# Expert weights of a decoder step loaded as rows of 2048 and 1536 columns, and a visit of two column groups in place of four blocks

## The reference, cut to what matters

```python
def swiglu(x, w_gate, w_up, w_down):
    return (jax.nn.silu(x @ w_gate) * (x @ w_up)) @ w_down

for e in range(N_EXPERTS):                       # 8 experts
    y_e = swiglu(xt, w_gate[e], w_up[e], w_down[e])
    y = y + combine[:, e:e + 1] * y_e
x = layer_norm(ALPHA * x + y, ln2_g, ln2_b)
```

## Time and profile before

| | |
|---|---|
| runs | 1489.25, 1490.39, 1491.16 us |
| profiled execution, span | 1489.3 us |
| what lies around the span | not recorded apart; the span is 1.1 us under the median of the runs |
| TensorE matmul busy | 1403.9 us, 94% |
| VectorE busy | 1323.4 us, 89% |
| ScalarE busy | 1104.7 us, 74% |
| loaded from HBM | 460.79 MB |
| mean granted TensorE clock | 0.986 |

### The profile page before, as it was taken

One profiled execution on the slowest core, in us unless ns is written; L12 is line 12 of the kernel. 1 busy time (PEld: TensorE's weight loads), 2 busy tenths in 40 slices (PEclk: granted clock), 3 DMA queues, 4 the chain that ended last, 5 costly groups with the idle time before them and its releaser, 6 DMA issues.

```text
span 1489.3 us, 39853 instructions
## 1 busy us (share of the span) xinstructions
PE 1403.9 (94%) x17570; PEld 1151.0 (77%) x17570; DVE 1323.4 (89%) x1315; ACT 1104.7 (74%) x1032; POOL 123.7 (8%) x162
## 2 busy tenths in 40 slices
PE   9999999999999999899999999999999898798786
PEld 7788878888788888697777788788877776766563
DVE  3999997555669999899999999999999999999997
ACT  4797755544458766688888878888878988978884
POOL 2411025000143001100000000000000000000001
PEclk9999999999999999999999999999999999999898
DMA  9654558456554637899999999999999999999993
GB/s 315 243 170 157 180 193 269 139 170 239 171 183 141 196 127 266 325 352 386 412 409 395 411 407 395 411 406 402 410 405 412 411 407 411 410 403 410 411 393 133
DMA packets 141347, 464.85 MB, mean 312 GB/s; under 512 B 8234, under 2 KB 10410, under 8 KB 126800
## 3 DMA queue, kind: packets, MB, share of 16 engines
q1 hardware_dynamic: 138960, 457.21, 80.4%
q0 software_dynamic: 1920, 4.55, 1.0%
q10 hardware_dynamic: 288, 0.48, 0.1%
HBM read 460.79 MB, written 2.89 MB: 311 GB/s over the span
## 4 chain that ended last, share of the span: by engine, by line
PE 52%; DVE 34%; DMA 5%; issue 5%; ACT 3%; POOL 1%; DVEq 0%; ACTq 0%
PE ps L869 16%; PE ps L870 16%; PE ps L871 16%; DVE w_lo L2284 14%; DVE w_lo L2287 7%; DMA stage<-in_moe_w_up 2%; PE ps L975 2%; DVE w_lo L1754 2%; ACT w_hi L1663 2%; DMA stage<-in_w_in 1%; DVE arena L1871 1%; DVE arena L1882 1%; POOL x L796 1%; DVE arena L2302 1%; DVE arena L2322 1%
## 5 line engine op out<-in xcount | busy, mean ns | idle before, releaser
L869 PE MATMUL ps<-arena,w_hi 128*128 128x128 f16 (+7 forms) x3952 | 564.5, 214 | 15.0 <-issue 10.1
L870 PE MATMUL ps<-arena,w_hi 128*128 128x128 f16 (+7 forms) x3952 | 564.3, 214 | 7.7 <-issue 7.7
L871 PE MATMUL ps<-arena,w_lo 128*128 128x128 f16 (+7 forms) x3952 | 564.3, 214 | 5.1 <-issue 5.1
L869 PEld LDWEIGHTS ps<-arena,w_hi 128*128 128x128 f16 x3952 | 386.1, 99 | 27.7 <-issue 15.8
L871 PEld LDWEIGHTS ps<-arena,w_lo 128*128 128x128 f16 x3952 | 386.2, 99 | 13.7 <-issue 8.3
L870 PEld LDWEIGHTS ps<-arena,w_hi 128*128 128x128 f16 x3952 | 386.2, 99 | 12.8 <-issue 4.8
L869 PE MATMUL ps<-xhl,w_hi 128*128 128x264 f16 x1088 | 300.4, 276 | 8.9 <-DVE xhl L1812 3.6
L871 PE MATMUL ps<-xhl,w_lo 128*128 128x264 f16 x1088 | 300.3, 276 | 0.0
L870 PE MATMUL ps<-xhl,w_hi 128*128 128x264 f16 x1088 | 300.3, 276 | 0.0
L1754 DVE SCALAR_TENSOR_TENSOR w_lo<-stage,w_hi 128x2048 f16<-128x2048 f32 (+1 forms) x94 | 209.1, 2246 | 80.9 <-ACT w_hi L1359 80.8
L1359 ACT ACTIVATE w_hi<-stage 128x2048 f16<-128x2048 f32 (+1 forms) x94 | 172.2, 1853 | 75.2 <-PE ps L871 62.0
(11 more groups left out here) (339 smaller groups left out, 1973.7 us busy)
## 6 DMA issues: line engine op xcount, KB each, us to landing
stage<-in_moe_w_up SPq DMA_DIRECT2D x64, 1024.0 KB, 14.0
stage<-in_moe_w_down SPq DMA_DIRECT2D x48, 1024.0 KB, 14.4
stage<-in_w_in SPq DMA_DIRECT2D x43, 1024.0 KB, 5.3
stage<-in_moe_w_gate SPq DMA_DIRECT2D x34, 1024.0 KB, 10.0
mixer_only<-in_moe_w_up SPq DMA_DIRECT2D x32, 1024.0 KB, 13.6
arena<-in_moe_w_gate SPq DMA_DIRECT2D x32, 1024.0 KB, 13.5
mixer_only<-in_moe_w_gate SPq DMA_DIRECT2D x23, 1024.0 KB, 13.5
mixer_only<-in_moe_w_down SPq DMA_DIRECT2D x16, 1024.0 KB, 14.3
```

What stands on the lines that cost most here:

```text
L869: mm(out, ah, bh, start=start, stop=False, skip_group_check=True)
L870: mm(out, ah, bl, start=False, stop=False, skip_group_check=True)
L871: return mm(out, al, bh, start=False, stop=stop, skip_group_check=True)
```

## The change

The seven column blocks form two groups, [0,1,2,3] and [4,5,6]. A gate or up piece is one k tile of 128 rows: 2048 columns (1 MB, 8 KB rows) in the first group, 1536 columns (768 KB, 6 KB rows) in the second. Down pieces stay as they are. A visit has 46 pieces: g0 in turns 0 to 7, u0 8 to 15, g1 16 to 23, six of d0 24 to 29, u1 30 to 37, the last two of d0 38 and 39, and d1 40 to 45. The high and low parts still have six slots and the ring still has 14 homes.

The four gate columns of group 0 take banks 0 to 3, and its four up columns the same banks after the silu; group 1 has banks 0, 1, 2 for gate and 3, 6, 7 for up. The readouts stand at fixed turns, each ahead of the split of piece q + 6: silu at 7 and 24, the product with up at 14 and 36, its high and low part at 16 and 38, the scattered sums at 8 and 11, the read of the gathered tokens at 38. The high part of a group is one instruction, and so is its low part (two each in a visit in place of four). The gather uses banks 0, 1, 2 and 3 and stands after u1, ahead of the last two d0 pieces, that is, ahead of eight down pieces. STRAIGHT is empty for every visit, so what the diff does with it does nothing here.

```diff
-BLOCKS = [[c for c in (b, b + 1) if c < NC] for b in range(0, NC, 2)]
-NB = len(BLOCKS)
...
+GROUPS = [[0, 1, 2, 3], [4, 5, 6]]
+NG = len(GROUPS)
+
+COLUMN_BANK = {("g", 0): [0, 1, 2, 3], ("u", 0): [0, 1, 2, 3], ("g", 1): [0, 1, 2], ("u", 1): [3, 6, 7]}
...
-    order = []
-    for b in range(NB):
-        order += [(kind, b, q) for kind in "gu" for q in range(n_pieces(b))]
-        if b:
-            order += [("d", b - 1, q) for q in range(n_pieces(b - 1))]
-    return order + [("d", NB - 1, q) for q in range(n_pieces(NB - 1))]
+    def run(kind, g, q0, q1):
+        return [(kind, g, q) for q in range(q0, q1)]
+
+    return (run("g", 0, 0, KT) + run("u", 0, 0, KT) + run("g", 1, 0, KT) + run("d", 0, 0, 6) + run("u", 1, 0, KT) +
+            run("d", 0, 6, 8) + run("d", 1, 0, 6))
...
+SILU_AT, UP_AT, HI_AT, LO_AT = (7, 24), (14, 36), (16, 38), (16, 38)
+ADD_AT, TURNED_AT, SELECT_AT, GATHER_AT = (8, 11), 17, 19, 38
...
-        silu_e = carve([2, 4 * CAP])
+        silu_e = carve([4, 4 * CAP])
...
-        yh = carve([D], F16)
-        yl = carve([D], F16)
+        yh, yl = [t[:, 0:2, :].rearrange("p a b -> p (a b)") for t in (hh, hl)]
...
+        def silu_taken(at, g, i):
+
+            return in_visit(bank_free, 0 if g or i < 2 else 2, at, 2 * g)
+
+        def up_taken(at, g, i):
+
+            if g:
+                return in_visit(bank_free, 6 if i else 3, at, 0)
+            return in_visit(bank_free, i // 2 * 2, at, 1)
...
-            width = 512 * len(BLOCKS[b])
-            k = KT // n_pieces(b)
-            return (w[0, e, q * k * P:(q + 1) * k * P, f:f + width]
-                    .rearrange("a (k p) n -> (a p) k n", p=P)), k, width
+            return (w[0, e, q * P:(q + 1) * P, f:f + width_of(m)]
+                    .rearrange("a (k p) n -> (a p) k n", p=P)), 1, width_of(m)
...
+                        elif i < RING:
+                            sp.wait_ge(*multiplied((r - 1, NE - 1), VISIT - 1))
                         else:
-                            sp.wait_ge(S["lo_done"], so_far((r, v), VISIT, split(n - RING + 1)))
-                        load(*visit_piece(e, m), n + v * VISIT + (0 if first else ROUND))
+                            sp.wait_ge(*home_left((r, (i - RING) // VISIT), (i - RING) % VISIT))
+                        src, tiles, width = visit_piece(e, m)
+                        dst = HOMES[home_of(r, i)][:, 0:tiles * width].rearrange("p (k n) -> p k n", k=tiles)
+                        sp.dma_start(dst, src).then_inc(landed_in(r, i)[0], 16)
...
+                turns = (((0, "gath_hi", xth, 6), (0, "gath_lo", xtl, 1), (1, "gath_hi", xth, 7), (1, "gath_lo", xtl, 3))
+                         if in_loop is None else
+                         ((0, "gath_hi", xth, 0), (1, "gath_hi", xth, 1), (0, "gath_lo", xtl, 2), (1, "gath_lo", xtl, 3)))
...
-                        if b != 6 or not first_visit(in_loop):
-                            pe.wait_ge(*{1: columns_read(1, in_loop, 2), 3: columns_read(3, in_loop, 2),
-                                         6: tokens_added(in_loop, 1), 7: in_visit(bank_free, 7, in_loop, 0)}[b])
+                        pe.wait_ge(*(up_taken(in_loop, 1, 0) if b == 3 else silu_taken(in_loop, 1, b)))
...
+            def columns_free(at, kind, g, i, b):
+
+                if (kind, g) == ("g", 0):
+                    if first_visit(at):
+                        pe.wait_ge(*in_visit(bank_free, b, at, -1))
+                    elif b == 0:
+                        pe.wait_ge(*in_visit(bank_free, 0, at, -1))
+                        pe.wait_ge(*in_visit(bank_free, 2, at, -1))
+                elif (kind, g) == ("u", 0):
+                    pe.wait_ge(*silu_taken(at, 0, i))
+                elif (kind, g) == ("g", 1) or b == 3:
+                    pe.wait_ge(*up_taken(at, 0, b))
+                elif b == 7:
+                    pe.wait_ge(*in_visit(bank_free, 7, at, 0))
+                elif not first_visit(at):
+                    pe.wait_ge(*tokens_added(at, 1))
...
+                        pe.wait_ge(*values_split(at, g))
+                        pe.wait_ge(S["lo_done"], split_done(at, m))
...
+                gate_up(at, "g", 1)
+                down(at, 0, 0, 6)
...
-                down(at, NB - 1)
+                down(at, 0, 6, 8)
+                down(at, 1, 0, 6)
...
+                for t, b in ((xgh, 0), (xgl, 2)):
+                    for h in range(2):
+                        act.wait_ge(*in_visit(bank_full, b + h, at, 3))
+                    fn(t[:, :, 0:cap].rearrange("p (h k) c -> p h k c", h=2),
+                       ps[:, b:b + 2, 0:4 * cap].rearrange("p h (k c) -> p h k c", k=4), ACT.Copy
+                       ).then_inc(bank_free[b], 1)
+
+            def silu(at, g):
+
+                cap = CAPS[at[1] % NE]
+                act.wait_ge(*values_free(at, g))
+                for b0, b1 in (((0, 2), (2, 4)), ((0, 3),))[g]:
+                    for b in range(b0, b1):
+                        act.wait_ge(*in_visit(bank_full, b, at, 2 * g))
+                    fn(silu_e[:, b0:b1, 0:4 * cap], ps[:, b0:b1, 0:4 * cap], ACT.Silu, scale=1 / WS
+                       ).then_inc(bank_free[b0], 1)
+
+            def values_hi(at, g):
+
+                cap = CAPS[at[1] % NE]
+                n = len(by_split(at[1], g))
+                if n:
+                    for i in range(n):
+                        act.wait_ge(*up_taken(at, g, i))
+                    fn(hh[:, 0:n, 0:4 * cap], h_e[:, 0:n, 0:4 * cap], ACT.Copy).then_inc(S["e_hi"], 1)
+                    for g in range(NG):
+                        if q == SILU_AT[g]:
+                            silu(at, g)
+                        if q == HI_AT[g]:
+                            values_hi(at, g)
+                    if q == GATHER_AT and at[1] < NE - 1:
+                        next_tokens(at)
+                    m = ahead(at[1], q)
+                    if m is not None:
+                        hi_v(at, m)
+
...
+            def up(at, g):
+
+                cap = CAPS[at[1] % NE]
+                banks = COLUMN_BANK["u", g]
+                for i0, i1 in (((0, 2), (2, 4)), ((0, 1), (1, 3)))[g]:
+                    dve.wait_ge(*silu_taken(at, g, i0))
...
+                        t = V.scalar_tensor_tensor(h_e[:, a:z_, 0:4 * cap], ps[:, banks[a]:banks[a] + z_ - a, 0:4 * cap],
+                                                   1.0 if straight[a - i0] else 1 / WS, silu_e[:, a:z_, 0:4 * cap],
+                                                   ALU.mult, ALU.mult)
+                    t.then_inc(bank_free[banks[i0]], 1)
...
+                    V.tensor_tensor(hl[:, 0:n, 0:4 * cap], h_e[:, 0:n, 0:4 * cap], hh[:, 0:n, 0:4 * cap],
+                                    ALU.subtract).then_inc(S["e_split"], n)
...
+                    if q in ADD_AT and not first_visit(at):
+                        scatter_add(at, ADD_AT.index(q))
+                    for g in range(NG):
+                        if q == UP_AT[g]:
+                            up(at, g)
+                        if q == LO_AT[g]:
+                            values_lo(at, g)
...
+                    m = ahead(at[1], q)
+                    if m is not None:
+                        lo_v(at, m)
```

More of the change, by code:

```diff
@@ L464, in so_far, with split_done, in_groups, hi_of @@
             return r * (NE * each) + (v * each + n)
+        def split_done(at, m):
+            r, v = at
+            return r * SPLIT_ROUND + (split(PRE) + SPLIT_BEFORE[v * VISIT + m + 1])
+        def in_groups(at, g, each, more):
+            r, v = at
+            counts = [(u, h, each(u, h)) for u in range(NE) for h in range(NG)]
+            return r * sum(n for _, _, n in counts) + (more + sum(n for u, h, n in counts if (u, h) < (v, g)))
+        def hi_of(v, g):
+            return min(1, len(by_split(v, g)))
+        def lo_of(v, g):
+            return len(by_split(v, g))
+        def values_split(at, g):
+            return S["e_split"], in_groups(at, g, lo_of, 1 + lo_of(at[1], g))
+        def values_free(at, g):
+            return S["e_split"], in_groups(at, g, lo_of, 1)
         def free_of(name):
@@ new lines, in as_loaded, with gate_up_tile, width_of, ahead @@
+        def as_loaded(where, width):
+            return where[:, 0:width].rearrange("p (c two) -> p two c", two=2)
+        def gate_up_tile(t, slot, i, j, width):
+            o = (j % 2) * (width // 2) + P * (2 * i + j // 2)
+            return t[:, slot, o:o + P]
+        def width_of(m):
+            kind, g, q = order[m]
+            return PIECE if kind == "d" else 512 * len(GROUPS[g])
+        def ahead(v, q):
+            i = v * VISIT + q
+            s = SPLIT_BEFORE[i] + SLOTS
+            return SPLIT_LIST[s] - v * VISIT if not is_straight(i) and s < SPLIT_ROUND else None
@@ L1230, in down @@
-            def down(at, blk):
-                cap = CAPS[at[1] % NE]
-                for q in range(n_pieces(blk)):
-                    m = order.index(("d", blk, q))
-                    slot = slot_of(m)
```

(28 more changed lines are left out.)

341 lines of the change are left out of this document (142 added, 199 removed).

## The result

The changed kernel takes 1523.55 us, the median of four runs (1522.03 to 1524.89), beside 1490.78 us for the kernel before in the same comparison (1489.25 to 1493.85). The ratio is 1.0216, with a 95% interval of 1.0201 to 1.023: it is 32.8 us slower. The profiled execution has a span of 1520.2 us, 30.9 more than before. The forecast was slower, by 15.6.

What follows compares the result with a forecast made beforehand. TensorE was taken to bound visits 0 and 2, VectorE the others, loads just at the end. Terms of +2.4 (visits 0, 2), +8.4 (1, 3, 4, 5), +0.9 (6), +2.1 (7) and +1.8 (clock) gave +15.6: run 1506.0 us, range 1491 to 1520.

Steps and rivals of the forecast that it cites:

- rival A: The forecast itself: down pieces that come late behind the product with up make the kernel 4 to 22 us slower; chance 0.62.
- VectorE's wait at the end of visit 4: At each end of a VectorE-paced visit, VectorE waits 2.4 us for high parts, in steps of 0.3 to 0.4.
- TensorE was to stand about 5 us ahead of the gather's last bank: Sign in the trace: TensorE idle about 5 us before that bank, with a lower granted clock behind it.
- The last low part to the first scaled result: End of visit 7: 10.0 us between the two in place of 4.3, which adds 5.7 us.
- waits for loads in visits 6 and 7: Faster loads give back what VectorE loses there to loads, about 1.2 + 3.8 = 5 us.
- with a silu and a product not quite covered I take 1.2 (0.3 to 2.5): Visits 0 and 2, bound by TensorE: its waits are paid directly, 1.2 us a visit, +2.4 together.
- The silu was priced by its slope: Between g0 and u0 TensorE waits for two silus, each at most 1.14 us for 1024 columns.
- visit 7 3.6 for 2.1: Last visit: +0.2 of work, -3.8 of load waits and +5.7 at the end make +2.1 us.
- The own work: VectorE's own instructions with the new piece sizes: +0.2 us a visit, +1.3 in all.
- The clock: Low TensorE clock after the idle time before the gather's last bank: 0.45 us in visits 1, 4, 5, 6; +1.8 (0 to 10).
- Rival D: Down pieces at 1.2 GHz for 3 to 7 us a visit, six visits losing 2.5 to 5 more: 1520 to 1535; chance 0.14.
- Rival B: The loads decide: TensorE reaches d1 early, the loads' 5 us stay won against +1.3 of work: 1487 us; chance 0.13.

Runs made afterwards that it cites:

- experiment 1: The changed kernel with VectorE's readouts of the counts (bank 2) moved ahead of two low parts at the start of visit 0: 1516.96 us.
- experiment 2: The changed kernel with the readout of the counts moved ahead and silu's table loaded early, before visit 0's first high part: 1514.41 us.
- experiment 7: The changed kernel with the counts read out earlier, silu's table loaded early, and group 1's product with up at turn 34, its split at 36: 1494.61 us.
- experiments 3: The changed kernel with group 1's product with up at turn 34 instead of 36 and its high and low part at 36 instead of 38: 1503.83 us.
- experiment 11: The kernel of experiment 7 with each gate and up piece loaded by two transfers of half its columns (4 and 3 KB rows), down pieces whole: 1500.81 us.
- experiment 10: The kernel of experiment 7 with every piece loaded by two transfers, gate and up halved by columns, down by partitions (64 each): 1796.82 us.

## Why the prediction was right or wrong

- **The side and the mechanism held.** The late run of down pieces (rival A) is the largest part: moving the product by two turns gives back 19.7 of 32.8 us, and adding such a wait to the kernel before costs 60.3. VectorE's wait at the end of visit 4 was to be 2.4 us and was 2.74, in steps of about 0.3. That it fits so well is in part luck: the six pieces that the forecast followed waited 1.98, and pieces 44 and 45, which it had at nothing, 0.76. TensorE was to stand about 5 us ahead of the gather's last bank and stood 2.7 there (2.6 to 6.0 in visits 1 and 3 to 6). The last low part to the first scaled result was to be 10.0 and was 10.2; waits for loads in visits 6 and 7 were to go and went; the rate was to be about 415 GB/s and was 415 in visits 4 to 6.
- **The step that failed is "with a silu and a product not quite covered I take 1.2 (0.3 to 2.5)", where it was applied to visit 0.** That visit lost 10.8 us, 9.6 more than forecast, out of the 15.3 by which the sum was short. I had listed which banks each group takes, but followed only the readouts that the change moves. The readout of the counts in bank 2 is older and stands in the code that leads into visit 0, and the banks that g0 newly takes made it urgent: 6.6 us (experiment 1). The silu was priced by its slope, 1.14 us for each half, without the table load ahead of the first one: 2.5 us (experiment 2). Both stand in front of TensorE in a visit that TensorE bounds, and the lower clock came with both.
- **The other visits were somewhat under-sized.** Visit 2 lost 3.4 for 1.2, and visit 7 3.6 for 2.1. Part of visit 2's is its boundary, since its window holds 1593 matmuls for 1560 before and that of visit 1 holds 1570 for 1604; what the rest is stays open. Visits 1 and 3 to 6 lost 14.3 where the terms, with the clock, gave 11.1. The own work was put at +0.2 a visit; VectorE's busy time in visit 4 grew by 0.76 (104.11 less 103.35), near the 0.7 of eight low parts that wait and don't overlap. With them back to back the same list takes 103.24 in experiment 7: the column arithmetic was right.
- **The clock was the second term that was mis-sized.** The forecast worked out 0.9 us for a stretch at 1.2 GHz behind the pause, then took half of it in each of visits 1, 4, 5 and 6: +1.8. The stretch came in all four, and in visit 4 did what was worked out: piece 38 took 1.7 us longer, and TensorE no longer waited for the split (0.8 us in visit 3). Visit 3, without a stretch, lost 2.3 us for 2.1; the other four lost 12.0 where the terms without the clock give 7.2. VectorE's waits for the high parts of pieces 44 and 45 are 1.9, 0.8, 1.2 and 1.2 us in these four and none in visit 3. Nor is the clock apart from the waits: the pauses of visit 0 brought their own 1.7 us each, and with the waits gone the mean is 0.986 in experiments 3 and 7, where it is 0.978 after. No run changed the clock by itself, so how much of the 4.8 us is the clock's stays open.
- **Rival D** had down pieces at 1.2 GHz for 3 to 7 us in each of six visits, for 2.5 to 5 us more each. In visits 1, 4, 5 and 6 the stretch behind the pause did fall on down pieces, but one of them was slowed in each (piece 38, by 1.4 to 1.9 us), and in visits 2 and 3, whose granted clock is 1.00 and which still lost 3.4 and 2.3 us, none. Its price did not come.
- **Rival B** (the loads decide) did not come about, but its premise is shown by experiment 11: longer rows are worth 6 us where VectorE is full. The Trainium skill (DMA: Bandwidth & Descriptors, SWDGE vs HWDGE vs iDMA) prefers packets of at most 4096 B. Taken as a rule for the rows of these loads, 6 and 8 KB would win nothing over 3 and 4 KB; the runs disagree, by 415 to 407 GB/s.

## What to carry to other kernels

When a change lets work use a buffer or bank that it did not use before, list every reader of that bank, those of the stage before too, and find each in its engine's in-order list: a readout of 0.16 us behind 4.5 us of unrelated work cost 4 us of its visit, and 6.6 by the medians. Place a readout that frees a bank by what waits for it and by how many slots run ahead: two turns too late cost 19.7 us, four too late 113, and in the last visit two turns too early cost 6.3. A pause of TensorE can cost twice: in visit 4 one of 2.7 us was followed by a down piece at half the clock, 1.7 us longer, on the same path. And measure a faster load where no other wait is left in the visit: there, in experiments 7 and 11, it was worth 6 us.

## What the runs showed of the hardware

- A transfer into 64 partitions runs at about half the rate of one into 128: 231 GB/s with 8 KB rows (experiment 10), against 415 for whole pieces; the median packet of 8 KB took 574 ns there and 311 in experiment 7. I had taken it for a neutral control. The Trainium skill (SBUF — State Buffer, Door 1: The DMA port swizzle) says that the rate depends on how many of the 16 ports the partitions reach, and partitions 0 to 63 reach half of them; the trace agrees.
- The time of a packet grows a little slower than its bytes: medians of 124, 160, 235 and 311 ns for 3, 4, 6 and 8 KB (experiments 7 and 11), 396 to 421 GB/s over 16 engines. Rows of 6 KB, which no row of before showed, come to 418, as the prediction took them.
